# Seven-product feed-forwards: the first panel's block products in another order, in other PSUM banks

## The reference, cut to what matters

```
def _swiglu(h, w_gate, w_up, w_down):
    return (jax.nn.silu(h @ w_gate) * (h @ w_up)) @ w_down
...
        h2 = _modulate(_rms_norm(x_new, norm2_g[l]), sh2, sc2)
        x_new = x_new + g2 * _swiglu(h2, w_gate[l], w_up[l], w_down[l])
...
        f = rmsnorm(h, pre_ff_g[l]) @ w_ff1[l]
        f = jnp.square(jax.nn.relu(f)) @ w_ff2[l]
        h = h + rmsnorm(f, post_ff_g[l])
```

## Time and profile before

| | us |
|---|---|
| median of 3 runs | 2500.69 |
| lowest and highest run | 2496.49, 2500.88 |
| time of the profiled execution | 2507.9 |
| span of the profiled execution | 2505.7 |
| PE busy in the span | 2392.7 (95%) |
| DVE busy | 1567.3 (63%) |
| ACT busy | 1036.3 (41%) |

### The profile page before, as it was taken

The page is one execution under the profiler, slowest core; times in us unless marked ns, Lnnn a source line. Parts: engine busy times, 40 slices in busy tenths (PEclk is TensorE's granted clock), DMA queues, the critical chain, the costliest instruction groups (busy, mean ns, idle before and its releaser), DMA issues.

```text
span 2505.7 us, 40944 instructions
## 1 busy us (share of the span) xinstructions
PE 2392.7 (95%) x15691; PEld 2050.3 (82%) x15691; DVE 1567.3 (63%) x2612; ACT 1036.3 (41%) x1972; POOL 258.0 (10%) x253
## 2 busy tenths in 40 slices
PE   5799999999898999999999999999979999999998
PEld 2798888788797888888888898899968888788886
DVE  3632327778768777777668923234287777666677
ACT  1422226676523332332444432433255444444444
POOL 0566310000101000000000100012040000000002
PEclk8899999999998999999999999999989999999999
DMA  9233330000331232232666421110313444477553
GB/s 322 70 118 117 118 84 9 2 2 27 110 127 68 81 126 93 97 125 77 228 198 199 162 68 43 35 35 35 135 68 111 167 139 156 147 256 235 151 176 118
DMA packets 191115, 290.32 MB, mean 116 GB/s; under 512 B 11736, under 2 KB 112028, under 8 KB 190620
## 3 DMA queue, kind: packets, MB, share of 16 engines
q1 hardware_dynamic: 190940, 287.94, 34.7%
HBM read 221.56 MB, written 67.34 MB: 115 GB/s over the span
## 4 chain that ended last, share of the span: by engine, by line
PE 66%; DVE 3%; DMA 2%; issue 1%; POOL 1%; ACT 1%; SPq 0%; POOLq 0%; DVEq 0%; ACTq 0%
PE ps L1519 9%; PE ps L1520 9%; PE ps L1521 9%; PE ps L1761 6%; PE ps L1762 6%; PE ps L1763 6%; PE ps L403 4%; PE ps L404 4%; PE ps L405 4%; PE ps L1982 1%; PE ps L1984 1%; PE ps L1983 1%; PE ps L1411 1%; DMA stage<-w_out 0%; PE ps L2554 0%
## 5 line engine op out<-in xcount | busy, mean ns | idle before, releaser
L403 PE MATMUL ps<-w_hi,ht_hi 128*128 128x256 f32 x1488 | 435.3, 293 | 21.2 <-DVE w_lo L388 14.8
L404 PE MATMUL ps<-w_lo,ht_hi 128*128 128x256 f32 x1488 | 426.6, 287 | 0.0
L405 PE MATMUL ps<-w_hi,ht_lo 128*128 128x256 f32 x1488 | 426.3, 287 | 0.0
L403 PEld LDWEIGHTS ps<-w_hi,ht_hi 128*128 128x128 f32 x1488 | 290.9, 196 | 42.8 <-issue 20.1
L404 PEld LDWEIGHTS ps<-w_lo,ht_hi 128*128 128x128 f32 x1488 | 291.4, 196 | 0.5 <-issue 0.5
L405 PEld LDWEIGHTS ps<-w_hi,ht_lo 128*128 128x128 f32 x1488 | 291.1, 196 | 0.0
L1761 PE MATMUL ps<-ff_b_hi,ff_a_hi 128*128 128x512 f32 x448 | 174.5, 390 | 3.3 <-issue 2.1
L1763 PE MATMUL ps<-ff_b_hi,ff_a_lo 128*128 128x512 f32 x448 | 174.3, 389 | 0.0
L1762 PE MATMUL ps<-ff_b_lo,ff_a_hi 128*128 128x512 f32 x448 | 174.3, 389 | 0.0
L1519 PE MATMUL ps<-ht_hi,swiglu_w_hi 128*128 128x512 f32 x352 | 137.3, 390 | 2.4 <-DVE swiglu_gate L1558 2.4
L1722 ACT ACTIVATE ff_a_hi<-ff_a_raw 128x512 fp32r<-128x512 f32 x112 | 70.7, 631 | 165.9 <-PE ps L1763 148.8
(11 more groups left out here) (371 smaller groups left out, 5792.0 us busy)
## 6 DMA issues: line engine op xcount, KB each, us to landing
ff_a_raw<-ff_act_dram SPq DMA_DIRECT2D x112, 256.0 KB, 2.8
stage<-w_in SPq DMA_DIRECT2D x23, 1024.0 KB, 5.3
swiglu_a_raw<-swiglu_act_dram SPq DMA_DIRECT2D x77, 256.0 KB, 2.9
stage<-w_mod SPq DMA_DIRECT2D x16, 1024.0 KB, 5.4
ff_stage<-w_ff SPq DMA_DIRECT2D x16, 1024.0 KB, 5.5
ff_act_dram<-ff_act_sums SPq DMA_DIRECT2D x16, 1024.0 KB, 4.3
ff_act_dram<-ff_acts SPq DMA_DIRECT2D x16, 768.0 KB, 5.8
swiglu_stage<-w_gate SPq DMA_DIRECT2D x11, 1024.0 KB, 6.3
```

What stands on the lines that cost most here:

```text
L403: pe.matmul(bank, a, wh[:, k, :], start=(k == 0), stop=False)
L404: pe.matmul(bank, a, wl[:, k, :], start=False, stop=False)
L405: mm = pe.matmul(bank, b, wh[:, k, :], start=False, stop=(k == KT - 1))
```

## The change

The first panel of each feed-forward makes its products in the order P1, P2, P3, P5, P7, P6, P4 (`FIRST`). P3 needs group 0 alone, which is turned from unmixed rows; P5 and P7 need `mix_first`'s two results; P6 needs `mix_second`, P4 `mix_third`. The groups are renumbered to that order: group 1 is P5's, 2 is P7's, 3 is P6's, 4 is P4's. The later panels keep their order.

- Banks: P3 goes to bank 2, P6 to bank 7, P4 to bank 4, P7 stays in 0 and waits for `keep`, P5 stays in 3. P3 and P4 of panel 0 no longer wait for a join. The last eight turns use banks 4 to 6 only. Panel 1's first four products wait for the joins of P5, P7, P2 and P3 of panel 0.
- The weights of P3 and P6 of panel 0 change their buffers with each other. P3's weights, not P6's, are split early, beside the dense layer, and so wait for `weight_sum(0, 3)`.
- PE: products stand before the last turn of their successor's group, as the diff shows. ACT: the weights of P7, P6 and P4, `keep` and the first weights of panel 1 stand between the high parts of groups 1 and 2. DVE: `mix_first(2)` and `mix_first(3)` move behind the last normalized rows, and the mixes are placed by hand among the low parts.

```diff
+        FIRST = (P1, P2, P3, P5, P7, P6, P4)
...
+            def late_at(e):
+                return 4 + (e % 4 if e < 12 else (e - 12) % 3)
...
-                    pe.wait_ge(f.mixed, f0.mixed + (8 + j + 1, 2 * j + 1, 2 * j + 2, 12 + j + 1)[g - 1])
-                pe.wait_ge(f.lo7, f0.lo7 + (3 + j // 2 if g == 0 else e + 1))
-                source = (half(4 + j, 1), half(4 + j, 1), half(j, 0), half(4 + j, 0), half(j, 1))[g]
+                    pe.wait_ge(f.mixed, f0.mixed + (2 * j + 1, 2 * j + 2, 8 + j + 1, 12 + j + 1)[g - 1])
+                held = [x for x in range(e) if late_at(x) == late_at(e)]
+                pe.wait_ge(f.lo7, f0.lo7 + (3 + j // 2 if g == 0 else 4 + held[-1] + 1))
+                source = (half(4 + j, 1), half(j, 0), half(4 + j, 0), half(4 + j, 1), half(j, 1))[g]
...
             def bank(q, b):
+                if q == 0:
+                    return ps[:, (0, 1, 7, 3, 0, 2, 4)[b], :]
                 return ps[:, (7 * q + b) % 4, :]
...
-                    pe.wait_ge(f.lo7, f0.lo7 + {P1: 4, P2: 4, P6: 12, P5: 16, P7: 20, P3: 8, P4: 24}[b])
-                if 7 * q + b >= 4:
+                    pe.wait_ge(f.lo7, f0.lo7 + {P1: 4, P2: 4, P3: 8, P5: 12, P7: 16, P6: 20, P4: 24}[b])
+                    if b == P7:
+                        pe.wait_ge(f.kept, f0.kept + 1)
+                elif q == 1 and b < 4:
+                    pe.wait_ge(f.joined, f0.joined + JOINED[(P5, P7, P2, P3)[b]])
+                else:
...
         def blocks_pe(pe, f, evac):
...
-            for g in (1, 2):
-                for j in range(4):
-                    f.turn_block(pe, g, j)
+            for j in range(3):
+                f.turn_block(pe, 1, j)
             pe.wait_ge(dense_evac, evac)
+            f.product(pe, 0, P3)
+            f.turn_block(pe, 1, 3)
+            for j in range(3):
+                f.turn_block(pe, 2, j)
+            f.product(pe, 0, P5)
+            f.turn_block(pe, 2, 3)
+            for j in range(3):
+                f.turn_block(pe, 3, j)
+            f.product(pe, 0, P7)
+            f.turn_block(pe, 3, 3)
+            f.turn_block(pe, 4, 0)
+            f.turn_block(pe, 4, 1)
             f.product(pe, 0, P6)
-            for j in range(4):
-                f.turn_block(pe, 3, j)
-            f.product(pe, 0, P5)
-            for j in range(4):
-                f.turn_block(pe, 4, j)
-            for b in (P7, P3, P4):
-                f.product(pe, 0, b)
+            f.turn_block(pe, 4, 2)
+            f.turn_block(pe, 4, 3)
+            f.product(pe, 0, P4)
...
         def blocks_act(act, f):
...
-            for b in (P7, P3, P4):
+            for b in (P7, P6, P4):
                 f.weight_hi(act, 0, b)
             f.tick_act(act, 0, P1)
+            for j in range(4):
+                f.block_hi(act, 2, j)
             f.tick_act(act, 0, P2)
-            for g in (2, 3, 4):
+            for g in (3, 4):
...
         def blocks_dve(dve, f):
 
+            f.mix_first(dve, 2)
             for j in range(4):
-                f.mix_second(dve, j)
                 f.block_lo(dve, 0, j)
+            f.mix_first(dve, 3)
             for j in range(4):
-                f.mix_third(dve, j)
                 f.block_lo(dve, 1, j)
-            for b in (P7, P3, P4):
-                f.weight_lo(dve, 0, b)
-            for g in (2, 3, 4):
-                for j in range(4):
-                    f.block_lo(dve, g, j)
+            f.weight_lo(dve, 0, P7)
+            for j in range(4):
+                f.block_lo(dve, 2, j)
+            f.mix_second(dve, 0)
+            f.mix_second(dve, 1)
+            f.block_lo(dve, 3, 0)
+            f.mix_second(dve, 2)
+            f.block_lo(dve, 3, 1)
+            f.mix_second(dve, 3)
+            f.block_lo(dve, 3, 2)
+            f.weight_lo(dve, 0, P6)
+            f.mix_third(dve, 0)
+            f.block_lo(dve, 3, 3)
+            f.mix_third(dve, 1)
+            f.block_lo(dve, 4, 0)
+            f.mix_third(dve, 2)
+            f.block_lo(dve, 4, 1)
+            f.mix_third(dve, 3)
+            f.weight_lo(dve, 0, P4)
+            f.block_lo(dve, 4, 2)
+            f.block_lo(dve, 4, 3)
...
-            for b in (P1, P2, P6, P5):
+            for b in (P1, P2, P3, P5):
                 f.weight_hi(act, 0, b)
...
             f1.weight_sum(dve, 0, 3)
-            f1.weight_lo(dve, 0, P6)
+            f1.weight_lo(dve, 0, P3)
             f1.weight_lo(dve, 0, P5)
...
             modulate(7)
-            f1.mix_first(dve, 2)
-            f1.mix_first(dve, 3)
             blocks_dve(dve, f1)
...
-                if j >= 7:
+                if j in (7, 8):
                     f2.mix_first(dve, j - 7)
             blocks_dve(dve, f2)
```

More of the change, by code:

```diff
@@ L1365, in late_block, with place_of, w_at @@
                     return (ht_hi, ht_lo)[part][:, 4:8, high]
-                if g == 2:
+                if g == 1:
                     return (ht_hi, ht_lo)[part][:, 0:4, high]
-                return (t_hi, t_lo)[part][(1, 3, 4).index(g)][:, :, cols]
+                return (t_hi, t_lo)[part][(3, 2, 4).index(g)][:, :, cols]
+            def late_at(e):
+                return 4 + (e % 4 if e < 12 else (e - 12) % 3)
             def bank_late(e):
-                return ps[:, 4 + e % 4, :].rearrange("p (k n) -> p k n", n=P)
+                return ps[:, late_at(e), :].rearrange("p (k n) -> p k n", n=P)
+            def place_of(q, b):
+                return 7 * q + (FIRST.index(b) if q == 0 else b)
+            def w_at(q, b):
+                return {P6: P3, P3: P6}.get(b, b) if q == 0 else b
             def half(j, k):
@@ L1406, in turn_block @@
                 else:
-                    pe.wait_ge(f.mixed, f0.mixed + (8 + j + 1, 2 * j + 1, 2 * j + 2, 12 + j + 1)[g - 1])
-                pe.wait_ge(f.lo7, f0.lo7 + (3 + j // 2 if g == 0 else e + 1))
-                source = (half(4 + j, 1), half(4 + j, 1), half(j, 0), half(4 + j, 0), half(j, 1))[g]
+                    pe.wait_ge(f.mixed, f0.mixed + (2 * j + 1, 2 * j + 2, 8 + j + 1, 12 + j + 1)[g - 1])
+                held = [x for x in range(e) if late_at(x) == late_at(e)]
+                pe.wait_ge(f.lo7, f0.lo7 + (3 + j // 2 if g == 0 else 4 + held[-1] + 1))
+                source = (half(4 + j, 1), half(j, 0), half(4 + j, 0), half(4 + j, 1), half(j, 1))[g]
                 for k in range(4):
-                    mm = pe.transpose(ps[:, 4 + e % 4, k * P:(k + 1) * P], source[:, k * P:(k + 1) * P], ident[:, :])
+                    mm = pe.transpose(ps[:, late_at(e), k * P:(k + 1) * P], source[:, k * P:(k + 1) * P], ident[:, :])
                 mm.then_inc(f.turned, 1)
@@ L1474, in weight_hi @@
                 if q:
-                    act.wait_ge(f.made, f0.made + 7 * (q - 1) + b + 1)
-                act.activation(w7_hi[b][:, :, :], w_source(q, b), ACT.Copy).then_inc(f.w_hi, 1)
+                    act.wait_ge(f.made, f0.made + place_of(q - 1, {P6: P3, P3: P6}.get(b, b) if q == 1 else b) + 1)
+                act.activation(w7_hi[w_at(q, b)][:, :, :], w_source(q, b), ACT.Copy).then_inc(f.w_hi, 1)
             def weight_lo(dve, q, b):
-                dve.wait_ge(f.w_hi, f0.w_hi + 7 * q + b + 1)
-                dve.tensor_tensor(w7_lo[b][:, :, :], w_source(q, b), w7_hi[b][:, :, :].bitcast(F32), ALU.subtract).then_inc(f.w_lo, 1)
+                dve.wait_ge(f.w_hi, f0.w_hi + place_of(q, b) + 1)
+                dve.tensor_tensor(w7_lo[w_at(q, b)][:, :, :], w_source(q, b), w7_hi[w_at(q, b)][:, :, :].bitcast(F32), ALU.subtract).then_inc(f.w_lo, 1)
             def weight_sum(dve, q, i):
@@ L1487, in weight_sum @@
                     if q:
-                        dve.wait_ge(f.w_lo, f0.w_lo + 7 * (q - 1) + 4)
+                        dve.wait_ge(f.w_lo, f0.w_lo + 7 * (q - 1) + (6 if q == 1 else 4))
                     out, x, y, op = w_s1[:, :, :], a21, a22, ALU.add
@@ L1518, in product @@
                 for k in range(4):
-                    pe.matmul(bank(q, b), w7_hi[b][:, k, :], x_of(0, b, k), start=(k == 0), stop=False)
-                    pe.matmul(bank(q, b), w7_hi[b][:, k, :], x_of(1, b, k), start=False, stop=False)
-                    mm = pe.matmul(bank(q, b), w7_lo[b][:, k, :], x_of(0, b, k), start=False, stop=(k == 3))
+                    pe.matmul(bank(q, b), w7_hi[w_at(q, b)][:, k, :], x_of(0, b, k), start=(k == 0), stop=False)
+                    pe.matmul(bank(q, b), w7_hi[w_at(q, b)][:, k, :], x_of(1, b, k), start=False, stop=False)
+                    mm = pe.matmul(bank(q, b), w7_lo[w_at(q, b)][:, k, :], x_of(0, b, k), start=False, stop=(k == 3))
                 mm.then_inc(f.made, 1)
@@ L1530, in keep @@
             def keep(act, q):
-                act.wait_ge(f.made, f0.made + 7 * q + P1 + 1)
+                act.wait_ge(f.made, f0.made + place_of(q, P1) + 1)
                 if q:
@@ L1541, in join @@
                 made = (P2, P6, P5, P7, P7, P3, P4)[i]
-                dve.wait_ge(f.made, f0.made + 7 * q + made + 1)
```

(3 more changed lines are left out.)

2 lines of the change are left out of this document (1 added, 1 removed).

## The result

The changed kernel takes 2528.93 us (median of 4 runs, 2526.68 to 2529.63) against 2500.78 before (median of 4 runs, 2496.49 to 2505.99); the ratio is 1.0102, with a 95% interval of 1.0084 to 1.0121. It is slower, as forecast, and by more: 28 us by the medians and 25.5 by the ratio (21 to 30 by its interval), where 16 were forecast and the range ended at 2524. A second measurement of both on one chip gave 1.0096 (1.0082 to 1.0110), that is 24 us.

A forecast was written before the change was run, and what follows sets the result against it. DVE's and ACT's queues were to bound the first panel, judged by PE's start of P1 of panel 1; 2.6 + 6.1 + 0.8 = 9.5 us plus 6.5 us gave 16.0 us, 2500.7 to 2516.7, range 2508 to 2524.

The forecast's parts named there:

- the range: Whole kernel: forecast time from 2508 to 2524 us, said to leave out about 2 in 10.
- Part 3: PE's clock: half-clock start of P1 of panel 1 costs 0.8 us in the first feed-forward, not counted in the second.
- Part 4: Second feed-forward: DVE waits of 12.0 to 13.0 us against 5.1 before; loss taken as 6.5 us.
- Part 1: First feed-forward, beside the dense layer: ACT's wait for P3's weights delays `modulate(5)` and all DVE work by 2.6 us.
- Part 2: First feed-forward, among the blocks: DVE waits of 10.0 us against 3.9 before, 6.1 us more.
- The front of the second feed-forward: Beside the dense layer: ACT's 1.3 us delay at 1821 is taken up by the dense layer's pace; counted at nothing.
- The low bound of the first feed-forward: Loss in the first feed-forward without any half clock in the new order: 7.9 us.

The follow-up runs named there:

- f_banks_only: Kernel before, order untouched, with banks 4 and 5 for P3 and P4 of panel 0 and none of their waits for joins; 1.0014 of the kernel before.
- e_fill: Changed kernel plus 20 matmuls whose results nothing reads, on PE between P4 of panel 0 and P1 of panel 1; 1.0069 of the kernel before.
- c_front: Changed kernel with `weight_sum(0, 3)` moved ahead of the merge and the normalized row it stood behind; 1.0085 of the kernel before.
- i_three: Changed kernel with turns before products, `weight_sum(0, 3)` early and 20 unread matmuls before P1 of panel 1; 1.0030 of the kernel before.
- h_mix3_first: Changed kernel with `mix_first(3)` on DVE ahead of group 0's low parts again; 1.0092 of the kernel before.
- g_best_again: Changed kernel's banks and product order, another hand-made order of turns, copies and mixes, `weight_sum(0, 3)` early; second measurement, 0.9985 of the kernel before.
- j_best_fill: Changed kernel's banks and product order, another hand-made order of turns, copies and mixes, plus 10 unread matmuls before P1 of panel 1; 0.9971 of the kernel before.
- after: The changed kernel as first measured and profiled, against the kernel before; 2528.93 us, ratio 1.0102.
- b_turns_ahead: Changed kernel with PE's order altered alone, all four turns of a group before the product; 1.0057 of the kernel before.
- d_act_order: Changed kernel with ACT's order altered alone, group 2's high parts before all of the copies but that of P7's weights; 1.0110 of the kernel before.

## Why the prediction was right in its mechanism and short in its size

**Right.** The direction, the bound (DVE's queue, PE judged at P1 of panel 1), the place of every new wait, and their sum in the first feed-forward (9.93 for 10.0 us; the list as it stands adds up to 9.8). Removing the waits of P3 and P4 for joins was worth nothing (f_banks_only). Queues carried forward by hand placed P1 of panel 1 at 825.5; it came at 825.11; two errors that cancel, in the front and in the waits, have a part in that (below). In the changed kernel the granted clock is 0.73 from 799 to 801 us, where PE had made only turns since P5, and P7 began at half rate. The Trainium skill, TensorE: Matmul & The Clock Gate, Part 4: PE-mode transpose, says that transposes don't count as PE being busy in the same way; the trace doesn't contradict it here, but PE also stood idle for 2.01 and 1.15 us between these turns, so the stretch of 9.2 us in the kernel before is the better witness.

```profile
799.00:801.00 2.00, 1.41 (x8) 1.18 (x8) 1.14 (x2) 0.51 (x1) 0.00 (x0) 0.73 0.00 0
```

**The terms that were mis-sized**, against 21.6 us in the four stretches (the sum was 16.0):
- *Part 3, the clock at P1 of panel 1:* this is the step that failed. It had 0.8 us in the first feed-forward and 0 in the second. Measured 2.5 and 1.4 to 2.9 (e_fill removes just these). I took the price from P6's row of the first feed-forward, 3.58 us, a product in whose first third the clock came back, and not the 4.51 of the second, and I left it out of the second feed-forward because the gap was half a microsecond shorter. P1 of panel 1 was in fact at half clock for its full length, 5.25 us in the first feed-forward, longer than either of the rows of before that I had. Short by about 3.8.
- *Part 4, the second feed-forward to panel 1:* 6.5. Its own list of waits gave 7 to 8, and 8.8 and 7.5 us were measured (47.0 and 45.7 for 38.2). I took 6.5, nearer to the lower of the two carried results (5.7 and 7.7). Short by 1.6.
- *Part 1, the front:* 2.6, measured 1.4 in the start of `modulate(5)` (773.34 for 771.94), 1.8 as c_front counts it. The square moved by 4.2 us as said (771.21 for 767.00), but from its start to the factor it was 2.1 us instead of 3.42: POOL's two operations, in the rows below (timeline of POOL in the changed kernel), took 0.19 and 0.59, where before they took 1.23 and 0.87 (the second in the earlier trace rows). Long by about 1.

```profile
772.43 0.19 POOL L1397 TENSOR_SCALAR swiglu_means<-swiglu_sums 128x1 f32<-128x1 f32 x1 [6.16 <-ACT junk L1393]
772.71 0.59 POOL L1399 TENSOR_TENSOR swiglu_roots<-swiglu_means,neg_half 128x1 f32<-128x1 f32 x1
...
779.27 1.23 POOL L1397 TENSOR_SCALAR swiglu_means<-swiglu_sums 128x1 f32<-128x1 f32 x1 [3.00 <-ACT junk L1393]
780.58 0.87 POOL L1399 TENSOR_TENSOR swiglu_roots<-swiglu_means,neg_half 128x1 f32<-128x1 f32 x1
```

- *Part 2, the first feed-forward's waits:* 6.1. Measured 6.4 against the first profile of before (9.93 less 3.53), and 7.5 against the second, whose waits sum to 2.44. Short by about 1, which Part 1 cancels: together they were to be 8.7, and the stretch to panel 1 grew by 8.8 (53.4 for a mean of 44.6).

These make 3.8 + 1.6 = 5.4 of the 5.6 us that the sum was short. The front of the second feed-forward, counted at nothing, cost nothing that shows: from the first down-projection to P1 of panel 0 of the second it is 645.3 and 643.5 us, before 645.5 and 647.3. The low bound of the first feed-forward, 7.9, doesn't follow from the list either, which gives 7.1 without half clock; nothing hangs on it.

**The range.** By the four stretches the kernel stands at 2500.7 + 21.6 = 2522.3, inside it. The timed difference is 24 to 28 us. The 2 to 6 us between are not explained: the part before P1 of panel 0 wanders by 8 us from execution to execution over all kernels, the part between the feed-forwards by 6, and in the two profiles of the changed kernel no stretch outside the four is longer in a way that repeats. I had taken the shift as exact on any base and gave nothing for this. Whether it is chance or a loss in a place that was not looked at stays open. The timed ratios of f_banks_only and i_three lie 4.8 and 3.8 us above their stretches; those of e_fill, h_mix3_first, g_best_again and j_best_fill agree with theirs to about 1 us.

Outside the four stretches one loss can be named; it is 1.5 of i_three's 3.8 us and has no part in the changed kernel's. From the second down-projection to the end it is 317.2 to 317.6 us in eleven profiles, and 319.0 and 318.9 in e_fill and i_three. PE has stood for 2.0 us before that down-projection in all of them. In seven (after, b_turns_ahead, h_mix3_first, f_banks_only, j_best_fill and these two) the clock then fell for about 3 us. In the others it held and PE waited 1.1 to 1.2 us for DVE a little later. Only e_fill and i_three have both, and they are the 1.5 us longer. The rows are e_fill's:

```profile
2199.64:2203.64 4.00, 4.00 (x12) 3.18 (x11) 3.62 (x6) 3.94 (x8) 0.00 (x0) 0.57 0.36 133
...
2215.20 0.47 PE L1778 MATMUL ps<-ff_b_hi,ff_a_hi 128*128 128x512 f32 x1 [1.11 <-DVE ff_b_lo L1766]
```

## What to carry to other kernels

Where one in-order queue meets three others, a late block is as late as the longest chain behind which it is queued: put the short operation that another engine waits for (here a 0.43 us turn) before the long one that nobody waits for (a 2.8 us product), and put independent work of the waiting engine into the gap. A wait removed from an engine that isn't the bound comes back where it next meets the bound one (f_banks_only), and a single DVE wait is not worth its own length while another stands behind it (d_act_order). Price a restart at half clock from the worst case, here a whole product at half clock (2.4 us more), at each gap that the change opens, and compare two profiles by stretches that begin at a common mark.
